# Column sums of a modulation vector: by turns on TensorE, or by accumulating transfers in memory and one transposition

## The reference

```python
mod = jax.nn.silu(c) @ w_ada + b_ada                   # 1 x 6144; w_ada is 1024 x 6144
shift1, scale1, gate1, shift2, scale2, gate2 = jnp.split(mod, 6, axis=-1)
h = modulate(rms_norm(x, g_norm1), shift1, scale1)     # start of the second block
...
x = x + (1 + gate1[:, None, :]) * mixed
h2 = modulate(rms_norm(x, g_norm2), shift2, scale2)
x = x + (1 + gate2[:, None, :]) * (...)
```

## Time and profile before

| | |
|---|---|
| median of 3 runs | 1409.38 us (1409.08 to 1410.72) |
| the profiled execution | 1409.77 us, of which the span 1408.1 us |
| PE busy | 1392.1 us (99%) |
| PE weight loads busy | 1148.8 us (82%) |
| DVE busy | 903.8 us (64%) |
| ACT busy | 606.4 us (43%) |
| POOL busy | 118.0 us (8%) |
| moved by transfers | 212.22 MB, 151 GB/s on average |
| chain that ended last, by engine | PE 83%, DVE 9%, ACT 3%, issue 2%, transfers 2% |

### The profile page before, as it was taken

How to read it: one execution, slowest core, us unless ns; L and a number is a source line. 1 busy time by engine, 2 the same in 40 slices (tenths; PEclk the granted TensorE clock), 3 DMA queues, 4 the chain that set the end, 5 groups by cost and what they waited for, 6 DMA issues and landing times.

```text
span 1408.1 us, 17288 instructions
## 1 busy us (share of the span) xinstructions
PE 1392.1 (99%) x6585; PEld 1148.8 (82%) x6585; DVE 903.8 (64%) x1243; ACT 606.4 (43%) x822; POOL 118.0 (8%) x135
## 2 busy tenths in 40 slices
PE   9999999999999899999999999999999999999998
PEld 8888888888888788888888877777799888888887
DVE  5555644677378664774855666667668664777693
ACT  6543322223224453543533445547545453544432
POOL 1000000000000213021000000000012002001120
PEclk9999999999999999999999999999999999999999
DMA  7244455446545798869452313030158729624621
GB/s 243 93 135 135 136 178 166 148 135 209 190 140 196 250 228 240 209 200 234 134 187 86 119 44 106 3 118 31 60 150 250 198 81 269 188 90 113 201 76 60
DMA packets 140418, 212.22 MB, mean 151 GB/s; under 512 B 3873, under 2 KB 104335, under 8 KB 139583
## 3 DMA queue, kind: packets, MB, share of 16 engines
q1 hardware_dynamic: 112992, 127.67, 28.0%
q0 software_dynamic: 26736, 83.21, 22.0%
q10 hardware_dynamic: 623, 0.43, 0.1%
HBM read 198.58 MB, written 7.48 MB: 146 GB/s over the span
## 4 chain that ended last, share of the span: by engine, by line
PE 83%; DVE 9%; ACT 3%; issue 2%; DMA 2%; DVEq 0%; ACTq 0%; POOL 0%; SPq 0%; POOLq 0%
PE bank L860 17%; PE bank L862 17%; PE bank L861 17%; PE aux L1080 14%; PE bank L1185 5%; DMA raw<-in_w_up 2%; DVE weights_lo L2037 2%; PE aux L1421 1%; PE bank L1421 1%; DVE ada_sums L2216 1%; PE bank L984 1%; PE bank L982 1%; PE bank L983 1%; ACT weights_hi L1467 1%; PE bank L1317 1%
## 5 line engine op out<-in xcount | busy, mean ns | idle before, releaser
L860 PE MATMUL bank<-operand_hi,weights_hi 128*128 128x512 f32 x1248 | 488.8, 392 | 1.1 <-DVE weights_lo L2037 0.8
L862 PE MATMUL bank<-operand_hi,weights_lo 128*128 128x512 f32 x1248 | 486.5, 390 | 0.0
L861 PE MATMUL bank<-operand_lo,weights_hi 128*128 128x512 f32 x1248 | 486.4, 390 | 0.0
L2037 DVE TENSOR_TENSOR weights_lo<-raw,weights_hi 128x1024 fp32r<-128x1024 f32 (+1 forms) x190 | 235.5, 1247 | 165.8 <-ACT weights_hi L1467 164.1
L860 PEld LDWEIGHTS bank<-operand_hi,weights_hi 128*128 128x128 f32 x1248 | 234.8, 188 | 51.2 <-DVE weights_lo L2037 1.8
L862 PEld LDWEIGHTS bank<-operand_hi,weights_lo 128*128 128x128 f32 x1248 | 234.7, 188 | 49.0
L861 PEld LDWEIGHTS bank<-operand_lo,weights_hi 128*128 128x128 f32 x1248 | 234.7, 188 | 48.1
L1467 ACT ACTIVATE weights_hi<-raw 128x1024 fp32r<-128x1024 f32 (+1 forms) x190 | 197.7, 1047 | 167.0 <-PE bank L862 65.2
L2216 DVE SCALAR_TENSOR_TENSOR ada_sums<-ada_or_attention,c_silu,ada_sums 128x384 f32<-128x384 f32 x112 | 69.2, 618 | 3.4
L1472 ACT ACTIVATE operand_hi<-value 128x512 fp32r<-128x512 f32 (+1 forms) x40 | 25.3, 633 | 99.6 <-DVE value L2271 39.0
L1951 ACT ACTIVATE conv_or_gate<-bank,vector_table 128x512 f32<-128x512 f32 x44 | 34.0, 773 | 68.1 <-PE bank L862 66.6
(11 more groups left out here) (404 smaller groups left out, 2075.9 us busy)
## 6 DMA issues: line engine op xcount, KB each, us to landing
raw<-in_w_in SPq DMA_DIRECT2D x39, 1024.0 KB, 5.3
raw<-in_w_ff SPq DMA_DIRECT2D x29, 1024.0 KB, 6.4
ada_or_attention<-in_w_ada POOLq DMA_DIRECT2D x16, 1536.0 KB, 7.9
raw<-in_w_up SPq DMA_DIRECT2D x22, 1024.0 KB, 6.6
x_features<-in_w_ff POOLq DMA_DIRECT2D x12, 1024.0 KB, 11.0
raw<-in_w_out SPq DMA_DIRECT2D x8, 1024.0 KB, 4.9
x_features<-in_w_down POOLq DMA_DIRECT2D x8, 1024.0 KB, 11.0
raw<-in_w_down SPq DMA_DIRECT2D x6, 1024.0 KB, 5.0
```

The source lines that it names most:

```text
L860: pe.matmul(dst[:, :], wh, ah, start=(kt == 0), stop=False)
L861: pe.matmul(dst[:, :], wh, al, start=False, stop=False)
L862: mm = pe.matmul(dst[:, :], wl, ah, start=False, stop=(kt == k_tiles - 1))
L2037: dve.tensor_tensor(lo[:, 0:k_tiles * P].rearrange("p (k n) -> p k n", n=P), src[:, :, k % 2 * P:(k % 2 + 1) * P], hi[:, 0:k_tiles * P].bi ...
```

## The change

All 16 pieces are saved to one array in memory, `sums_dram` of 128 x 6144 (`save_sums`, each behind the load of the next piece on POOL's queue). There the partition sum is made by halving: four accumulating transfers add rows 64 to 127 to rows 0 to 63, then 32 to 63 to 0 to 31, and so on, until 8 rows are left (`halve`, levels 64, 32, 16, 8). One is issued in each of the three feed-forward rounds of POOL and one after them. The 8 rows are loaded back as 48 partitions of 8 x 128 (`mod_parts`), DVE adds the eight in one reduction (`mod_rows`, 48 x 128), and PE transposes them once into 128 x 48. PE waits for that reduction ahead of quad `ff`+7. All six vectors are then made at once. The turns between tiles, DVE's reductions of them, and the matmuls with ones go.

In the phases `xs`, `pb` and `out` DVE sums its piece at the head of the quad, ahead of tile 0, all eight steps together. In the other phases the piece stays behind tiles 1 and 2. Before its first step DVE waits until the piece has landed and the sums before it are saved. The quads of `ga` to `gb` are plain loops on PE now.

```diff
@@ POOL
-            with pool.Fori(0, ADA_NOW + 1) as piece:
-                load_ada(piece)
-            for piece in range(ADA_NOW + 1, 16):
-                load_ada(piece)
-                save_late(piece - 1)
-            save_late(15)
+            def save_sums(piece):
+
+                pool.dma_start(sums_dram[:, bass.ds(piece * ADA, ADA)], acc[:, :]).then_inc(ada_saved, 16)
+
+            load_ada(0)
+            with pool.Fori(0, ADA_PIECES - 1) as piece:
+                load_ada(piece + 1)
+                save_sums(piece)
+            pool.wait_ge(ada_step, 1 + KT * ADA_PIECES)
+            save_sums(ADA_PIECES - 1)
+
+            def halve(level):
+
+                pool.wait_ge(ada_saved, 16 * ADA_PIECES)
+                if level > 0:
+                    pool.wait_ge(ada_halved, 16 * level)
+                n = LEVELS[level]
+                lower, upper = (sums_dram[e * n:(e + 1) * n, :].rearrange("p (j n) -> p j n", n=2 * D) for e in range(2))
+                pool.dma_start(lower, upper, accum_op=ALU.add, max_dma_last_dim=4096).then_inc(ada_halved, 16)
...
                 add_quarters(r, t1_raw, (0, 1), t1_landed)
                 add_to_t2(2, (0, 1))
+                if r in FF_ROUNDS:
+                    halve(r)
                 add_quarters(r, t3_raw, (1, 1), t3_landed)
...
             for r in FF_ROUNDS:
                 weight_sums(r)
+            halve(3)
...
-            pool.wait_ge(late_saved, 6 * 16)
-            pool.dma_start(late_acc, late_dram[:, :]).then_inc(late_back, 16)
+            pool.wait_ge(ada_halved, 16 * len(LEVELS))
+            pool.dma_start(mod_parts.rearrange("q (r c) -> q r c", c=P),
+                           sums_dram[0:LEVELS[-1], :].rearrange("r (q c) -> q r c", c=P)).then_inc(ada_back, 16)
@@ PE
-                pe.wait_ge(late_back, 16)
-                turn_late_sums(ADA_LATE[0])
...
-            first_quads_and_ada()
-            quads_and_ada("pa", 1, MADE["u"], 1)
-            quads_and_ada("cg", 0, MADE["n1"], 3)
-            quads_and_ada("xs", 0, MADE["n1"], 5)
-            quads_and_ada("bg", 0, MADE["n1"], 7)
...
+            quads("ga", 0, MADE["n1"])
+            quads("pa", 1, MADE["u"])
+            for name in ("cg", "xs", "bg", "gb"):
+                quads(name, 0, MADE["n1"])
...
                 stream(F["ff"] + 6, (k,), 1)
                 if k >= 2:
                     turn_y(k - 2)
+            pe.wait_ge(ada_reduced, 1)
+            pe.transpose(aux[3][:, 0:NMOD * KT], mod_rows, ident[0:NMOD * KT, 0:NMOD * KT]).then_inc(mod_turned, 1)
             stream(F["ff"] + 7, (0, 1), 1)
...
             sum_squares("n3")
-            turn_late_sums(ADA_LATE[1])
             spread_rms("n3")
-            turn_late_sums(ADA_LATE[2])
@@ DVE
                 if kts[0] == 0:
                     dve.wait_ge(ada_landed, 16 * (piece + 1))
...
+                    if not (isinstance(piece, int) and piece == 0):
+                        dve.wait_ge(ada_saved, 16 * piece)
...
+            def quad(name, i, work, after, piece=None, own_weights=False, at_head=False):
+
+                if at_head:
+                    ada(piece + i, range(KT))
...
+            phase("xs", product(to_value, lambda n: tile(gates, n)), taps, piece=6, at_head=True)
...
+            phase("gb", None, piece=10)
+            phase("pb", product(to_value, lambda n: tile(gates, n)), add_kept, piece=12, at_head=True)
...
+                quad("out", i, grow_x, split_and_sum, 14, own_weights=True, at_head=True)
...
             last_first_layer(0)
-            dve.wait_ge(ada_kept, ADA_NOW)
-            modulation(0, 3, 0, C_G1, 2, 0)
+            dve.wait_ge(ada_back, 16)
+            dve.tensor_reduce(mod_rows, mod_parts.rearrange("q (r c) -> q c r", c=P), mybir.AxisListType.X,
+                              ALU.add).then_inc(ada_reduced, 1)
+            modulation()
...
-                    if n == 0:
-                        dve.wait_ge(ada_turned, ADA_NOW + 3)
-                        modulation(3, 6, 1, C_G2, 3, 4)
```

More of the change, by code:

```diff
@@ L377, in build @@
         mixed, mix_biased, tap0, tap1, tap2 = (sem(n) for n in ("mixed", "mix_biased", "tap0", "tap1", "tap2"))
-        ada_landed, ada_step, ada_turned, ada_kept, mod_done = (
-            sem(n) for n in ("ada_landed", "ada_step", "ada_turned", "ada_kept", "mod_done"))
-        mod_begun = sem("mod_begun")
+        ada_landed, ada_step, ada_saved, ada_halved, ada_back, ada_reduced, mod_turned, mod_done = (
+            sem(n) for n in ("ada_landed", "ada_step", "ada_saved", "ada_halved", "ada_back", "ada_reduced", "mod_turned",
+                             "mod_done"))
         silu_done = sem("silu_done")
@@ L2192, in _, with ada @@
             dve.wait_ge(table_kept, 3)
-            def keep_ada(pieces):
-                dve.wait_ge(ada_turned, pieces)
-                dve.tensor_reduce(ada_cols[:, bass.ds(3 * pieces - 3, 3)], aux[2][:, 0:ADA].rearrange("p (m n) -> p m n", n=P),
-                                  mybir.AxisListType.X, ALU.add).then_inc(ada_kept, 1)
-            def ada(piece, kts, late=False):
+            def ada(piece, kts):
                 sums = acc[:, :]
@@ L2205, in ada @@
                     dve.wait_ge(ada_landed, 16 * (piece + 1))
-                    if late and piece > ADA_NOW:
-                        dve.wait_ge(late_saved, 16 * (piece - ADA_NOW))
-                    elif not (isinstance(piece, int) and piece == 0):
-                        keep_ada(piece)
+                    if not (isinstance(piece, int) and piece == 0):
+                        dve.wait_ge(ada_saved, 16 * piece)
                 for kt in kts:
@@ L2219, in _ @@
             ADA_PART = {1: range(0, 4), 2: range(4, KT)}
-            def quad(name, i, work, after, piece=None, own_weights=False):
+            def quad(name, i, work, after, piece=None, own_weights=False, at_head=False):
+                if at_head:
+                    ada(piece + i, range(KT))
                 for k in range(4):
@@ L2230, in quad, with phase @@
                         weights(q + 1, k)
-                    if piece is not None and k in ADA_PART:
-                        ada(piece + i, ADA_PART[k], isinstance(i, int) and piece >= ADA_NOW)
-            def phase(name, work, after=None, piece=None):
+                    if piece is not None and k in ADA_PART and not at_head:
+                        ada(piece + i, ADA_PART[k])
+            def phase(name, work, after=None, piece=None, at_head=False):
                 with dve.Fori(0, 2) as i:
-                    quad(name, i, work, after, piece)
+                    quad(name, i, work, after, piece, at_head=at_head)
             def all_but_last_square(name):
@@ L2281, in _ @@
             phase("cg", None, piece=4)
-            phase("xs", product(to_value, lambda n: tile(gates, n)), taps, piece=6)
+            phase("xs", product(to_value, lambda n: tile(gates, n)), taps, piece=6, at_head=True)
             phase("bg", gate_conv, lambda n, q, k: rest(1, n, tA[k % 2][:, :], MADE["bg"] + n), piece=8)
-            for i in range(2):
-                quad("gb", i, None, None, ADA_NOW)
-            for i in range(2):
-                quad("pb", i, product(to_value, lambda n: tile(gates, n)), add_kept, ADA_NOW + 2)
+            phase("gb", None, piece=10)
+            phase("pb", product(to_value, lambda n: tile(gates, n)), add_kept, piece=12, at_head=True)
             clear_sum()
@@ L2303, in _ @@
             for i in range(2):
-                quad("out", i, grow_x, split_and_sum, ADA_NOW + 4, own_weights=True)
+                quad("out", i, grow_x, split_and_sum, 14, own_weights=True, at_head=True)
             sum_by_token("n2")
```

82 lines of the change are left out of this document (21 added, 61 removed).

## The result

| | before | changed |
|---|---|---|
| median | 1409.74 us (1409.08 to 1410.72) | 1418.58 us (1416.52 to 1418.65) |
| profiled execution | 1409.77 us, span 1408.1 us | 1416.52 us, span 1415.0 us |
| mean granted clock | 0.998 | 0.996 here, 0.993 in the three other executions |

A forecast was written before the change was run, and what follows sets the result against it. The prediction took TensorE (PE), busy for 99% of the span, as the bound. Its terms, -2.9 + 3.2 + 1.1 - 5.2 + 1.2 + 5.1 + 1.5 + 0.8 = +4.8 us on 1409.4, gave 1414.2 us, range 1409.0 to 1418.0.

The forecast's parts named there:

- the sum's signs: Signs of the eight summed terms: -2.9, +3.2, +1.1, -5.2, +1.2, +5.1, +1.5 and +0.8 us, together +4.8 us.
- `xs`: Term for summing pieces at the heads of `xs`: DVE delivers low weights late and `bg` starts later, +3.2 us.
- Turns: Term for the ten turns between tiles removed: 0.36 us of PE each, eight counted, -2.9 us.
- The `n2` wait and its clock: Term for heads of `out`: PE's 3.54 us wait before `n2` square sums and 1.7 us of low clock go, -5.2 us.
- that heads cost nothing: Rival in `xs` and `pb`: DVE enters both phases without delay, giving 1408.9 us; chance 0.18.
- That the clock holds: Rival at the transposition and `n3`: idle stretches without a clock fall in one or both, 1412.7 or 1411.2 us; chance 0.22.
- That the wait on `ada_reduced` is short: Rival ahead of `ff`+7: DVE reaches the reduction before PE gets there, 5.1 and 1.5 us go, 1407.6 us; chance 0.07.
- the clock behind the transposition: Term behind PE's wait on `ada_reduced`: the granted clock falls after 4.8 us idle, +1.5 us (0 to +3).
- `n3`: Term for fillers removed at `n3`: chain starts 0.7 us earlier, clock may fall (+1.5 us, six in ten), +0.8 us.
- the heads of `pb`: Term for summing pieces at the heads of `pb`: low weights for `pb` and `out` come late, +1.1 us.
- the transfers: Term for the four accumulating transfers: in round 1 the weight load loses time to the second one, +1.2 us (0 to +8.1).
- The rival of the starved load: Rival in round 1: larger packets of the transfers delay the weight load, +4.8 in place of +1.2 us, 1417.8 us; chance 0.15.

The follow-up runs named there:

- the second profile: The changed kernel run once more with no edit: profiled execution 1416.49 us at a clock of 0.993, median 1417.15 us, ratio 1.0055.

## Why the prediction was right and wrong

**Right: the direction, the sum's signs, and most mechanisms.** PE lost 5.2 us ahead of the transposition, with DVE's reduction ending just before it; `ff`+7 started 28.3 us behind `ff`+6, 5.7 us later than before, where 5.1 were forecast. The half microsecond is the reduction, taken as 1.3 us by its 1024 values against the 512 of the earlier trace rows. It took 1.85 (timeline of DVE):

```profile
736.89 1.85 DVE L2427 TENSOR_REDUCE kept<-kept 48x128 f32<-48x1024 f32 x1
```

`xs` came out to a tenth: waits of 2.04 and 2.08 us, where 2.1 and a start of `bg` 48.0 us behind `xs` (measured 48.1) were worked out from the landing time of a save. Turns cost 0.36 us each. The `n2` wait and its clock went together, and more went than forecast (5.8 for 5.2). Of the rivals, that heads cost nothing is false: in `xs` and `pb` they cost 6.1 us against the same kernel without them, and come back only through `out`. That the clock holds is false: both stretches at the lower clock are in both profiles of the changed kernel, and in all others in which nothing fills or moves the two waits. That the wait on `ada_reduced` is short is false too (5.17 us).

**The steps that failed** are sizes of terms and not the mechanism: the clock behind the transposition (+1.5 us; 1.5 to 2.8 measured), `n3` (+0.8; 0.9 to 2.3), the heads of `pb` (+1.1; 2.3 to 2.8), and an upper end of the range that left no room for them together. The second median of the same kernel, 1417.15 us, lies inside the range: the miss is no larger than what the kernel's own executions differ by.

**Wrong: the terms of the clock.** The forecast gave +1.5 us for the clock behind the transposition, and +0.8 for `n3`, of which 1.5 was clock. Behind the transposition 1.5 us (seven matmuls at 0.427 us) is only the small case; 13 of them, with 2.8 us lost, were seen in the second profile. `n3` came to 1.6 us, 0.8 more than forecast: 13 matmuls at the lower clock are 2.6 us. I took the one low stretch of before as the size of each, eight matmuls, where these stretches ran from six to 14. The ends that I kept for the first (0 to 3) held; those for `n3` did not: it had none above +0.8.

**Wrong: the heads of `pb`**, +2.4 us for +1.1. The load of piece 12 is issued 1.1 us behind the start of `pb`, not 0.6 as before, and its save lands 0.2 us later than taken, so the first tile on DVE comes 14.5 us behind PE's start where 13.7 was worked out; the second quad's weights and those for `out` carry that along. DVE's timeline shows the save as what it waits for ahead of the sums:

```profile
383.50 0.42 DVE L2175 TENSOR_SCALAR ada_sums<-ada_or_attention,c_silu 128x384 f32<-128x384 f32 x1 [6.32 <-DMA modulation_sums<-ada_sums]
```

**Sized well but with the wrong spread: the transfers.** +1.2 us was forecast, the kernel without them says 0.1 to 2.3, so the value stands, in part by luck: it was a choice ("less than half of the shorter figure"), and the prices that it was chosen from were too low. The first transfer was put at 8.7 to 17.4 us and landed in 21.3, the second at 4.4 to 8.7 and landed in 16.4. The rival of the starved load has its mechanism right (packets of unequal size in equal numbers) and its size wrong: it took the 4.4 us of the second transfer as lost in full, and the load landed 2.0 us later. That its time, 1417.8, is the case nearest to the result is luck: it gave these transfers 4.8 us, and they cost 1.5 in the profiled execution.

**The range.** 1414.2 against 1418.58: of the 4.4 us between them, 1.3 are `pb`, 0.8 `n3`, 0.6 the transposition with the shorter low stretch, 0.3 the transfers; less 0.6 at `out` and 0.4 behind the mixer, this is the profiled execution (1416.52 us against a profiled 1409.77). The other 2.4 us are 2.1 by which the other executions are longer, and 0.4 by which the profiled execution of before lay above the median of 1409.38 us that the forecast started from, less rounding. The upper end of 1418.0 came from single cases, each priced alone; several clock terms at their upper ends at once were not among them.

## What to carry to other kernels

A wait can cost more than it lasts, through the clock behind it, and both go if a step is moved behind work that the engine has anyway: six row tiles of matmuls ahead of one transposition were worth 7.9 to 9.3 us, all that the change had lost. In this kernel, summing at the head of a stage paid only where the buffer's next load could start most of a stage earlier; put such a step one stage ahead of where it is needed (`pb` for `out`), and no earlier (`xs`). A transfer that is off every path still takes its share of the engines by the size of its packets: put it where the other queue has few loads, and ask what is next in its own queue.

## What the runs showed of the hardware

- A stretch at the lower clock behind the same wait doesn't have the same length in each execution: with those at its two ends counted in, six to 13 matmuls at about 0.427 us behind the transposition (wait 5.2 us), none to 14 in `xs` behind waits of 1.9 to 3.1 us, seven to 14 behind `n3`. Waits of 2.0 to 2.2 us were followed by the lower clock in some executions and not in others.
- Filling a wait with matmuls kept the clock at 1.00 in one case (4.2 us of fills ahead of the reduction), and in another (at `n3`) the clock fell over the fills themselves.
- An accumulating transfer from memory to memory of 1.5 MB took 19.2 to 21.9 us among the rounds' other transfers, 13.3 at the end of round 0 and 15.0 behind round 2; one of 192 KB took 3.5 to 6.5 us.
